# Scale broadcasts moved, and the first unit and x loaded and split in four pieces by K tiles

## What is computed

```python
def first_block(x, mem, ...):
    mem_n = rmsnorm(mem, mem_norm)
    for l in range(DEPTH):                      # 2 layers
        x = x + 0.5 * swiglu(rmsnorm(x, ffn1_norm[l]), ...)      # 1024 -> 2816 -> 1024
        h = rmsnorm(x, mix_norm[l])
        x = x + (even_mixer(h, ...) if l % 2 == 0 else odd_mixer(h, ...))
        x = x + memory_cross_attention(rmsnorm(x, xa_norm[l]), mem_n, ...)
        x = x + 0.5 * swiglu(rmsnorm(x, ffn2_norm[l]), ...)
    return rmsnorm(x, final_norm)

def second_block(x, p, ...):                    # 1 layer
    h = h + 0.5 * _swiglu(_rmsnorm(h, ffn1_norm[i]), ...)
    z = _rmsnorm(h, mix_norm[i]) @ w_in[i]      # convolution branch, gated linear attention
    h = h + jnp.concatenate([y_conv, y_gla], axis=-1) @ w_out[i]
    h = h + 0.5 * _swiglu(_rmsnorm(h, ffn2_norm[i]), ...)
    h = h + jax.nn.sigmoid(_rmsnorm(h, ple_norm[i]) @ ple_w_gate[i]) * (p[i] @ ple_w_proj[i])
    return _rmsnorm(h, final_norm)
```

## Time and profile before

| what | us |
|---|---|
| timed runs | 1645.86, 1649.97, 1652.22 |
| median | 1649.97 |
| profiled execution | 1650.46 |
| its span, first to last instruction | 1648.6 |
| TensorE busy | 1586.8 |
| VectorE busy | 1137.2 |
| ScalarE busy | 825.7 |

### The profile page before, as it was taken

The page is one execution under the profiler, slowest core; times in us unless marked ns, Lnnn a source line. Parts: engine busy times, 40 slices in busy tenths (PEclk is TensorE's granted clock), DMA queues, the critical chain, the costliest instruction groups (busy, mean ns, idle before and its releaser), DMA issues.

```text
span 1648.6 us, 23827 instructions
## 1 busy us (share of the span) xinstructions
PE 1586.8 (96%) x9065; PEld 1378.2 (84%) x9065; DVE 1137.2 (69%) x1613; ACT 825.7 (50%) x1148; POOL 73.4 (4%) x139
## 2 busy tenths in 40 slices
PE   6999999999999999999998999989999999999997
PEld 5888888888888888889977888868888898788885
DVE  6766648757766676666566876767666786776666
ACT  6554435545454555454444555545454641555454
POOL 3000002000000000000000900000000000000000
PEclk9999989999999999999999999999999999999999
DMA  8655534344655465554443455545655450465551
GB/s 287 228 189 193 158 123 154 128 162 151 224 182 200 135 224 178 204 178 155 152 154 103 138 197 201 179 145 196 212 177 189 132 179 26 135 230 188 194 182 48
DMA packets 209277, 280.58 MB, mean 170 GB/s; under 512 B 5166, under 2 KB 184792, under 8 KB 209208
## 3 DMA queue, kind: packets, MB, share of 16 engines
q1 hardware_dynamic: 206832, 274.50, 49.6%
q0 software_dynamic: 1360, 3.80, 0.7%
q10 hardware_dynamic: 1016, 1.32, 0.2%
HBM read 278.55 MB, written 2.63 MB: 171 GB/s over the span
## 4 chain that ended last, share of the span: by engine, by line
PE 84%; DVE 10%; ACT 4%; issue 1%; DMA 1%; DVEq 0%; SPq 0%; ACTq 0%
PE bank L1449 35%; PE bank L1500 28%; PE bank L1499 12%; DVE w_lo L882 4%; PE bank L1502 2%; PE bank L1879 2%; ACT w_hi L497 2%; PE bank L1556 1%; PE bank L1682 1%; ACT xT L525 1%; PE bank L1664 1%; DMA raw<-in_ffn_w_gate 1%; DVE x L969 0%; PE bank L1671 0%; DVE arena L1096 0%
## 5 line engine op out<-in xcount | busy, mean ns | idle before, releaser
L882 DVE TENSOR_TENSOR w_lo<-raw,w_hi 128x1024 fp32r<-128x1024 f32 x518 | 620.0, 1228 | 260.5 <-ACT w_hi L497 260.1
L1500 PE MATMUL bank<-xT,w_hi 128*128 128x512 f32 x2112 | 739.6, 399 | 12.1 <-DVE arena L990 5.8
L497 ACT ACTIVATE w_hi<-raw 128x1024 fp32r<-128x1024 f32 x518 | 529.5, 1051 | 147.2 <-PE bank L1500 84.5
L1499 PE MATMUL bank<-xT,w_lo 128*128 128x256 f32 x1848 | 519.0, 281 | 0.0
L1500 PEld LDWEIGHTS bank<-xT,w_hi 128*128 128x128 f32 x2112 | 385.3, 189 | 89.6 <-DVE w_lo L882 6.7
L1499 PEld LDWEIGHTS bank<-xT,w_lo 128*128 128x128 f32 x1848 | 350.9, 190 | 12.9
L1449 PE MATMUL bank<-w_hi,hid_hi 128*128 128x512 f32 x528 | 207.4, 393 | 0.0
L1449 PE MATMUL bank<-w_hi,hid_lo 128*128 128x512 f32 x528 | 205.6, 389 | 0.0
L1449 PE MATMUL bank<-w_lo,hid_hi 128*128 128x512 f32 x528 | 205.4, 389 | 0.0
L1449 PE MATMUL bank<-xT,w_hi 128*128 128x256 f32 x800 | 148.5, 288 | 0.8 <-DVE xT L922 0.6
L1449 PEld LDWEIGHTS bank<-xT,w_hi 128*128 128x128 f32 x800 | 126.3, 194 | 3.4 <-issue 3.1
(11 more groups left out here) (256 smaller groups left out, 1641.0 us busy)
## 6 DMA issues: line engine op xcount, KB each, us to landing
raw<-in_ffn_w_up SPq DMA_DIRECT2D x44, 1024.0 KB, 5.4
raw<-in_ffn_w_down SPq DMA_DIRECT2D x44, 1024.0 KB, 5.5
raw<-in_ffn_w_in SPq DMA_DIRECT2D x44, 1024.0 KB, 5.1
raw<-in_ffn_w_gate SPq DMA_DIRECT2D x43, 1024.0 KB, 5.4
raw<-in_ffn_w_out SPq DMA_DIRECT2D x22, 1024.0 KB, 5.4
raw<-in_w_in SPq DMA_DIRECT2D x10, 1024.0 KB, 5.3
raw<-in_xa_w_kv SPq DMA_DIRECT2D x8, 1024.0 KB, 4.9
raw<-in_od_w_in SPq DMA_DIRECT2D x8, 1024.0 KB, 5.5
```

The lines of the kernel that those rows point to most:

```text
L497: act.activation(hi, src, ACT.Copy).then_inc(sem["hi_ready"], 1)
L882: dve.tensor_tensor(lo, src, hi.bitcast(F32), ALU.subtract).then_inc(sem["lo_ready"], 1)
L1499: pe.matmul(bank[:, b, T:2 * T], lo, xT_hi[:, k, :], start=False, stop=False)
L1500: last = pe.matmul(bank[:, b, :], hi, xT[:, k, :, :], start=k == 0, stop=k == KD - 1)
```

## The change

Six edits.

1. SyncE issues, in this order: the first gate unit's K tiles 0 to 3 (both halves, rows of 256 columns), columns 0 to 511 of x (both row tiles), K tiles 4 to 7 of the unit, columns 512 to 1023 of x.
2. ScalarE and VectorE split each gate half of the first unit in two parts, K tiles 0 to 3 and 4 to 7, with the xT copies between them. The mean squares, the root and the diagonal of x come behind the splits of the up unit.
3. TensorE transposes K tiles 0 to 3 of x when its second piece is there, 4 to 7 when the fourth is; then both gate halves over K tiles 0 to 3, both over 4 to 7, the first up half, the broadcast, the second up half. VectorE takes the scale copy at the head of step 0 in this FFN.
4. In the other FFNs the broadcast leaves `opening` and stands ahead of the second half of step 1; in the late FFN ahead of the fourth. On VectorE the up sum stands ahead of the second split in step 0, and the scale copy behind it.
5. In the late FFN the two norms move into step 0: first split and gate sum, then the first norm (`first_norm`), up sum and split, then the second root and the diagonal (`second_norm`). ScalarE's second squares move behind its copies of the gate and up parts.
6. First mixer: the broadcast goes ahead of `transposed`, and VectorE splits one half ahead of the scale copy. Second block's mixer: the broadcast goes behind the last quarter of q, the first column unit ahead of the rank matmul, and VectorE splits one half ahead of the scale copy.

```diff
                 if u == 0:
-                    sp.dma_start(dst[:, :, 0:P], src[:, :, 0:P]).then_inc(sem["first_half_loaded"], 16)
-                    sp.dma_start(dst[:, :, P:UC], src[:, :, P:UC]).then_inc(raw_ready[slot], 16)
+                    x_rows = a["x"][0].rearrange("(t p) d -> p t d", p=P)
+                    sp.dma_start(dst[:, 0:4, :], src[:, 0:4, :]).then_inc(sem["first_part_loaded"], 16)
+                    sp.dma_start(x[:, :, 0:512], x_rows[:, :, 0:512]).then_inc(sem["x_loaded"], 16)
+                    sp.dma_start(dst[:, 4:KD, :], src[:, 4:KD, :]).then_inc(raw_ready[slot], 16)
+                    sp.dma_start(x[:, :, 512:D], x_rows[:, :, 512:D]).then_inc(sem["x1_loaded"], 16)
                     return
...
@@ ScalarE, start @@
-            split()
+            act.wait_ge(sem["first_part_loaded"], 16)
+            first_split(0, early, "first_hi_ready")
+            xT_his(COL_OF["ffn1"], xT_hi, ks=range(4))
+            first_split(1, early, "first_hi_ready")
+            xT_his(COL_OF["ffn1"], xT_hi, ks=range(4, KD))
+            act.wait_ge(raw_ready[0], landed[0])
+            for v in range(2):
+                first_split(v, late, "hi_ready")
+            v_next[0] = 2
+            splits(2)
             act.wait_ge(sem["x_loaded"], 16)
             act.wait_ge(sem["x1_loaded"], 16)
-            norm(COL_OF["ffn1"], loaded=True)
-            splits(LEAD - 1)
+            mean_square(0)
+            mean_square(1)
+            splits(LEAD - 4)
             memory_squares()
...
@@ VectorE, step 0 of an FFN @@
                 if j == 0:
+                    if first:
+                        scale_copy(4)
                     split(i, base)
                     gate_sum()
+                    if late:
+                        first_norm()
+                    up_sum()
                     split(i, base + 1)
-                    up_sum()
-                    scale_copy(4)
+                    if late:
+                        second_norm()
+                    if not first:
+                        scale_copy(4)
                     gate_scale()
                     up_scale()
...
@@ VectorE, start @@
+            first_split(0, early, "first_hi_ready", 1, "first_lo_ready")
+            xT_los(COL_OF["ffn1"], xT_hi, xT_lo, ks=range(4))
+            first_split(1, early, "first_hi_ready", 2, "first_lo_ready")
+            xT_los(COL_OF["ffn1"], xT_hi, xT_lo, ks=range(4, KD))
+            for v in range(2):
+                first_split(v, late, "hi_ready", v + 1, "lo_ready")
+            v_next[0] = 2
+            splits(2)
+            rstd_of_both()
+            diagonal()
+            splits(LEAD - 4)
             memory_scale()
-            end = ffn()
+            end = ffn(first=True)
...
@@ VectorE, first mixer @@
+            split()
             scale_copy(5)
-            for n in range(2):
-                scaled(v + 2 + 2 * n, q_sb[:, 2 * n:2 * n + 2, :], n)
-                splits(2)
+            scaled(v + 2, q_sb[:, 0:2, :], 0)
+            split()
+            scaled(v + 4, q_sb[:, 2:4, :], 1)
+            splits(2)
...
@@ TensorE @@
-                        if j == 1 and n == 1 and late:
+                        if j == 1 and n == (3 if late else 1) and not loaded:
                             scale_broadcast(4)
...
                 if loaded:
-                    for n in range(4):
-                        if n == 3:
-                            scale_broadcast(4)
-                        wide(v0 + n, n, None, first=n == 0)
+                    for ks in (range(4), range(4, KD)):
+                        for n in range(2):
+                            pe.wait_ge(sem["lo_ready" if ks[0] else "first_lo_ready"], n + 1)
+                            for k in ks:
+                                if n == 0:
+                                    c.next("xT_lo_ready")
+                                last = wide_product(n, n, k)
+                            if ks[0]:
+                                last.then_inc(sem["half_done"], 1)
+                    wide(2, 2, None)
+                    scale_broadcast(4)
+                    wide(3, 3, None)
                 else:
-                    opening(range(v0, v0 + 4), lambda n, k: wide_product(v0 + n, n, k),
-                            None if late else lambda: scale_broadcast(4))
+                    opening(range(v0, v0 + 4), lambda n, k: wide_product(v0 + n, n, k))
...
             two_units()
-            v = take()
-            transposed(v, bank[:, 2, 0:T], X)
             scale_broadcast(5)
+            transposed(take(), bank[:, 2, 0:T], X)
...
+            q_part(1, range(4, KD)).then_inc(sem["half_done"], 1)
             scale_broadcast(7)
-            q_part(1, range(4, KD)).then_inc(sem["half_done"], 1)
+            col_unit(6, X)
             c.next("proj_sb")
```

96 lines of the change are left out of this document (48 added, 48 removed).

## The result

The changed kernel took 1638.66 us (median; 1637.11 to 1639.14, 4 runs), the kernel before 1648.7 (1645.86 to 1652.22, 4 runs; the fourth came with the changed kernel's): ratio 0.9932, 95% interval 0.9917 to 0.9947. That is 10.0 us faster, more than the 8.2 us that the forecast took as the least that can be told, and 4.3 us above the forecast of 1634.4. On the chip of a later group of runs the two stood at 1638.2 and 1650.21 (0.9927, 0.9911 to 0.9944).

The account below looks back on a forecast made before the run. TensorE, busy 1586.8 of 1648.6 us, was taken to bound the kernel, leaving its idle time and its 1.2 GHz stretches to win. Terms 6.3 + 8.9 + 0.2 + 0 + 0.7 = 16.1 took 1650.5 to 1634.4 us; range 1629 to 1642.

Parts of the forecast that it names:

- Step 1: Start, first FFN: pieces of x land sooner, so memory transposes begin at 26.4 instead of 32.68, saving 6.3 us.
- the 12.5: Start: a first product later than 12.5 us would show the forecast wrong; it was expected at 10.9.
- the even 366 GB/s: Start: the four pieces' 2.1 MB move at 366 GB/s from about 2.1 us on, done at 7.9.
- Step 2: First mixer: no wait before `natural` (2.44 us) and the clock stays up there and behind it, together 8.9 us saved.
- Step 3: Late FFN: the 5.80 us wait moves to the fourth half's w_lo, low clock behind it; 0.2 us saved, bounds 0 to 2.5.
- Step 4: Second, third, fourth, sixth FFN openings: new waits of 0.2 to 0.3 us each offset 1.14 us gone; 0, bounds -3 to +1.
- Step 5: Second mixer: broadcast wait falls from 1.82 to 0.15 us, one new wait of about a microsecond; 0.7 us saved.
- a clock that falls in `natural`: Rival, first mixer: the clock falls there all the same, leaving that part worth 2.4 us, total 1640.9; chance 0.16.
- survive the late wait: Rival, late FFN: the clock stays up behind the moved wait, 2.3 us more saved, total 1632.1; chance 0.08.
- land in turn: Rival, start: pieces arrive one after another, the fourth at 16.0, the start worth 0.6 us, total 1640.1; chance 0.04.
- The start worth half: Rival, start: products on time, but the memory's scaling holds the transposes; worth 3 us, total 1637.7; chance 0.09.
- The slower one: Rival, four other FFN openings: a 10 us chain makes each wait 4.1 us with low clock behind, total 1660; chance 0.03.

Follow-up runs that it names:

- mixer_only: The kernel before with only the first mixer's edit (broadcast one half earlier, one VectorE split ahead of the scale copy): 1642.07 us, ratio 0.9958.
- mixer_half: The changed kernel, but in the first mixer VectorE splits late again while the broadcast stays early: 1638.69 us.
- late_split: The changed kernel, but in the late FFN the fourth half is split ahead of the scale copy and the broadcast stands one half earlier: 1632.9 us, ratio 0.9906.
- best_interleaved: The fastest kernel (`best`), but TensorE transposes columns 512 to 1023 of x behind the products over K tiles 0 to 3: 1632.4 us.
- best: The changed kernel with the late FFN's split and broadcast one half earlier, other FFN openings as before, and bias table loaded later: 1629.71 us, ratio 0.9879.

## Why the prediction was right, and where it was off

Sign and order of size were right; the time was 4.3 us above the forecast, within the range. By its own steps, from the profiled executions:

| step | forecast | measured |
|---|---|---|
| 1. start | 6.3 | 5.5 |
| 2. first mixer | 8.9 | 9.1, less 0.9 behind attention's stop |
| 3. late FFN | 0.2 | 1.4 to 1.5 (about 0 in other executions) |
| 4. other openings | 0 | -1.7 |
| 5. second mixer | 0.7 | -0.2 |
| sum | 16.1 | 13.4 |

*Step 1* has one step that failed and a margin that hid most of it. The fourth piece was put at 9.0 and landed at 11.1, so the first product came at 12.75, past the 12.5 that the forecast had named as the point at which it is wrong. What failed is the even 366 GB/s: the forecast had seen small transfers only as a margin, and the table's packets took 1.6 us of the 2.1. All links of the chain that ends in the scale copy then came 1.9 to 2.1 us late: the squares began at 16.88 (forecast 14.8), the diagonal was done at 21.9 (19.8), the copy at 26.95 (25.1). The transposes began at 27.09 where the bare sum had 25.1, and the 1.3 us set aside for a landing that slips left 0.7. With the table load late they began at 25.54, so the chain itself was sized well. (The forecast's "four quarters and two halves" of splits should read two quarters and two halves, 2.9 us; its 14.8 counts those.)

The low clock at the start was mis-sized too, but without effect. It was put at 5.4 us and measured at 2.9 (12.75 to 15.7). Nor is 5.4 a property of that start: `mixer_only`, whose start is that of before, had 2.7 us of slow products ahead of the stop where `before` had 5.2. In the eight executions with the changed start whose fourth piece landed at 11.1 to 11.3 the slow stretch was 1.4 to 3.1 us, and the transposes began at 27.09 to 27.29 in all of them, after a wait of 0.5 to 1.6 us for the scale copy. TensorE was not what was late.

*Step 2* held in every point: no wait, granted 1.00, 5.5 us for `natural`, the broadcast without a wait. The reason given was too narrow: not the early split alone does it (`mixer_half`). The 0.9 us lost behind attention's stop come from a longer slow stretch, 6.8 us and not 3.4; eight of the twelve experiments have the short one behind the same stop, so that is no effect of the change.

*Step 3*: the new wait was forecast at 5.8 us and measured 5.57, at the forecast's place and for the forecast's reason. The term mis-sized is the clock behind it, put at 5.1 us as before and measured at 2.9 to 3.5 in five profiles and 6.2 in two.

*Step 4* is where the range of the term (-3 to +1) was needed. The waits of 0.2 to 0.3 us came as worked out (0.25 in the row at 384.00; 0.30 to 0.37 us by the undoing). What failed is the 1.14 us at 918.17, which were to pay for them. VectorE is late in the fourth FFN because its root runs at half speed: from the first operation to the diagonal it takes 4.0 us there (900.26 to 904.24) and 2.2 at the start (19.25 to 21.42), and the 1.8 between them are more than the whole wait. Moving the broadcast away left the split and the gate sum behind the same root, and TensorE waits 1.58 us for them instead. VectorE's root there in the changed kernel, and the window around it:

```profile
902.81 0.31 DVE L914 TENSOR_TENSOR small<-small 128x2 f32<-128x2 f32 x1
...
899.00:905.00 6.00, 6.00 (x36) 5.14 (x34) 5.51 (x15) 2.69 (x4) 5.91 (x15) 1.00 0.00 0
```

*Step 5*: one wait of about a microsecond for a w_lo was forecast, and 0.32 + 0.81 came; the broadcast's wait stayed at 0.37 instead of 0.15 (1.82 - 1.6 makes 0.2). The stops make 1.50 us where there were 1.82, and yet the mixer as a whole is 0.2 longer. The rows around the stops have the 0.5 us between: a stop costs more than its bracket says. From 1294.90 to 1295.50 are 0.60 us, where such starts otherwise lie 0.12 apart; 0.32 of them are in the bracket and 0.16 are not, and the first matmul behind the stop takes 0.22 to the next start instead of 0.12. The stop at 1308.08 has the same 0.26 us around it. Two stops more than before make 0.52. The forecast priced a stop by its bracket alone.

Of the 4.3 us 2.7 are the sum's; the other 1.6 come from the profiled execution being the fastest of its four. What a stop does to the clock changes from execution to execution by 1 to 1.5 us at each of some four stops (2.07 us near 200, 2.28 in attention, 2.69 near 865, 5.57 in the late FFN), as much as most of the terms.

Of the rivals, a clock that falls in `natural` did not come, in any of the twelve profiles without the stop. The clock did not survive the late wait: it was down behind it in all seven profiles that have the wait. The pieces did not land in turn: the fourth was there at 11.1, not at 16.0. (The forecast's two reckonings of that case do not match: if 16.0 leaves 0.6 us of part 1, 13.6 leaves 3.0 and not 2.) The start worth half did not come either. The slower one did not: its waits are there, but 0.25 us and not 4, and the clock did not notice them.

## What to carry to other kernels

A stop costs more than its length where sparse work follows it: 2.44 us cost 9. A stop also costs some 0.26 us around its bracket (second mixer), so one wait cut into three is no gain. Look behind each wait for the granted clock before pricing it, and remove the whole stop, by whichever end of its chain is the easier to move. When a wait is moved, ask which engine is late: a broadcast moved away from a late VectorE left the next product waiting for the same VectorE (fourth FFN), and only work taken out from behind the long chain (`late_split`) made a wait of 5.6 us go. Transposes that feed three engines go first, even where TensorE could start on products.

## What the runs showed of the chip that was not expected

- A transfer of 1 KB in 4-byte elements on another queue lowered what all queues moved from 374 to 224 GB/s for 2.2 us. It was in the kernel before as well (222 GB/s), where the forecast took it for the price of short rows.
- The same stop of 2.07 us near 200 brought the clock down for 3.4 us in 5 of 14 profiled executions and left it up in 9, at a cost of 1.5 us. The longer stop of 2.69 us near 865 (878 before) left it up in 2 of the 14 (`mixer_only`, `best_interleaved`), and the one of 2.28 in none. Behind a stop of 5.57 it was down for 2.9 to 3.5 us or for 6.2. A single profile can't price such a stop; the medians of four runs scatter by as much.
- VectorE's operations on 128 x 2 elements took 0.31 to 0.37 us in the fourth FFN, in both kernels. GpSimd is busy for 5.91 of 6.00 us there, multiplying tiles of 128 x 128. The changed kernel's trace has 165 such operations while GpSimd does nothing, and none took over 0.18. Three more run beside GpSimd's products of 128 x 512 in the first mixer; they took 0.68 to 1.24 us, and each ended 0.02 us after GpSimd's, as here (1.30 us from 254.63, 1.24 from 254.71):

```profile
254.63 1.30 POOL L431 TENSOR_TENSOR arena<-arena,scale_row 128x512 f32<-128x512 f32 x1 [4.22 <-ACT arena L610]
...
254.71 1.24 DVE L1098 SCALAR_TENSOR_TENSOR small<-small 128x2 f32<-128x2 f32 x1
```

  Beside GpSimd's copies of 8 x 1 elements, in `best`, 19 of them took 0.16 to 0.21. The Trainium skill (GPSIMD Engine Reference, Specifications) says that GpSimd shares its memory interfaces with VectorE and gets in the way of some of its instructions. These rows agree. No run here moved GpSimd's work, so what it would give back in the fourth FFN is open.
